# Two mixer layers and an expert block on one core: head 0's q and k turned beside the last projection tiles, scores ahead of head 1's turns

## What is computed

```python
parts = split_in(h @ w_in[l])                      # 21 tiles of 128 columns, and kr
q = mla_q(parts[0], ...); k, v = mla_kv(parts[1], parts[2], ...)   # head norm and rope, 96 wide
z = dwconv(a * sigmoid(g), cf_conv_w) + cf_conv_b
z = silu(layer_norm(z, cf_ln_w, cf_ln_b))
y_c = (z @ cf_pw_w + cf_pw_b) * silu(g_c)
attn = attend(q, concat([kc, k]), concat([vc, v]))  # softmax(q k^T / sqrt(96)) v, per head
x_new = x + gate * (concat([attn * silu(g_a), y_b, y_c]) @ w_out[l])
```

## Time and profile before

| | |
|---|---|
| median of 3 runs | 1403.42 us (1402.58 to 1404.14) |
| the profiled execution | 1405.23 us, its span 1403.4 us, granted clock 0.962 |
| busy: PE, DVE, ACT, POOL | 1301.7, 671.7, 516.1, 581.0 us |
| layer 0: last three tiles, attention | about 254 to 294, 294 to 412 us |
| layer 1: last three tiles, attention | about 637 to 665, 665 to 768 us |

### The profile page before, as it was taken

One profiled execution on the slowest core, in us unless ns is written; L12 is line 12 of the kernel. 1 busy time (PEld: TensorE's weight loads), 2 busy tenths in 40 slices (PEclk: granted clock), 3 DMA queues, 4 the chain that ended last, 5 costly groups with the idle time before them and its releaser, 6 DMA issues. The chain is left out here.

```text
span 1403.4 us, 20309 instructions
## 1 busy us (share of the span) xinstructions
PE 1301.7 (93%) x7696; PEld 940.2 (67%) x7696; DVE 671.7 (48%) x1368; ACT 516.1 (37%) x1062; POOL 581.0 (41%) x599
## 2 busy tenths in 40 slices
PE   4999999989999899989899999999989799999985
PEld 3766877768888877656788987776667653333332
DVE  5456975137751588852675341444353711111216
ACT  4312343246752333523665343565452211111102
POOL 2113698334445446794244431564343311111125
PEclk8999999979999999999899999999989899999998
DMA  8792101130003231112000322221035939999974
GB/s 325 280 338 91 46 31 60 46 150 2 1 24 128 63 114 55 45 61 75 16 2 2 121 91 70 89 98 46 31 125 202 423 125 418 424 425 414 418 317 196
DMA packets 42655, 210.08 MB, mean 150 GB/s; under 512 B 7271, under 2 KB 9703, under 8 KB 33328
## 3 DMA queue, kind: packets, MB, share of 16 engines
q1 hardware_dynamic: 34336, 195.11, 36.3%
q0 software_dynamic: 5760, 10.27, 2.0%
q10 hardware_dynamic: 2448, 3.21, 0.7%
HBM read 201.98 MB, written 17.30 MB: 156 GB/s over the span
## 5 line engine op out<-in xcount | busy, mean ns | idle before, releaser
L436 POOL TENSOR_TENSOR wlo<-raw,whi 128x512 fp32r<-128x512 f32 x112 | 149.7, 1342 | 151.0 <-ACT whi L424 145.6
L3310 PE MATMUL ps<-gu,XT 128*64 128x512 f32 x608 | 136.5, 597 | 5.1 <-DVE XT L3408 3.4
L424 ACT ACTIVATE whi<-raw 128x512 fp32r<-128x512 f32 x124 | 76.5, 628 | 171.9 <-PE ps L872 132.7
L872 PE MATMUL ps<-hxh,whi 128*128 128x512 f32 x304 | 131.0, 431 | 5.0 <-DVE tmpc L1176 4.0
L1138 DVE SCALAR_TENSOR_TENSOR z<-glu,small,z 128x798 f32<-128x798 f32 (+1 forms) x120 | 128.3, 1120 | 0.7
L872 PE MATMUL ps<-hxh,wlo 128*128 128x512 f32 x304 | 121.7, 400 | 1.9 <-POOL wlo L436 1.9
L872 PE MATMUL ps<-hxl,whi 128*128 128x512 f32 x304 | 121.7, 400 | 0.0
L1491 PE MATMUL ps<-kT,qT 96*128 96x256 f32 (+1 forms) x432 | 97.2, 365 | 7.4 <-ACT qT L1537 7.1
L1648 POOL TENSOR_SCALAR P<-P,stat 128x768 f32<-128x768 f32 (+1 forms) x80 | 65.5, 821 | 89.9 <-DVE stat L1610 89.0
L3310 PEld LDWEIGHTS ps<-gu,XT 128*64 128x64 f32 x608 | 45.9, 137 | 82.8 <-issue 75.9
L1546 ACT ACTIVATE P<-ps,stat 128x768 f32<-128x768 f32 (+1 forms) x80 | 65.1, 814 | 66.7 <-DVE stat L1603 66.2
(11 more groups left out here) (846 smaller groups left out, 3096.6 us busy)
## 6 DMA issues: line engine op xcount, KB each, us to landing
gu<-in_w_gu_dram SPq DMA_DIRECT2D x32, 2048.0 KB, 16.4
raw<-in_w_in_dram SPq DMA_DIRECT2D x66, 512.0 KB, 3.4
dn<-in_w_dn_dram SPq DMA_DIRECT2D x32, 1024.0 KB, 16.5
wgate<-in_w_mod_dram SPq DMA_DIRECT2D x16, 1024.0 KB, 8.2
raw<-in_w_out_dram SPq DMA_DIRECT2D x24, 512.0 KB, 3.4
wmod<-in_w_mod_dram SPq DMA_DIRECT2D x4, 2048.0 KB, 13.5
ybuf<-zero SPq DMA_DIRECT2D x1, 4096.0 KB, 12.6
yin<-ybuf SPq DMA_DIRECT2D x4, 1024.0 KB, 8.8
```

What stands on the lines that cost most here:

```text
L424: e.activation(K.hi[i][:, half(h)], K.raw[i % 2][:, half(h)], ACT.Copy).then_inc(*q.up("hi", i, h))
L436: e.tensor_tensor(K.lo[i][:, half(h)], K.raw[i % 2][:, half(h)], K.hi[i][:, half(h)].bitcast(F32), ALU.subtract).then_inc(*q.up("lo", i, h))
L872: p = e.matmul(s[0:m, o:o + n], a, K.h[l, v][x][:, k, :], start=k == 0 and part == 0 and x == 0, stop=end)
L3310: m = e.matmul(s[o, :], x[:, k, o], gu[:, k, :], start=k == 0, stop=k == KT - 1, skip_group_check=True)
```

## The change

- In the job `norm` head 0's k is turned in gap 2 and its q in gap 5 (`turn_pe`), each in one place of `K.px` and as one piece (768 columns, for q in layer 1 512). ScalarE writes the high parts in gaps 3 and 6, VectorE the remainders in gaps 3 and 6, there behind the diagonals. `qs` is computed in gap 1.
- In layer 0 the spread stays in gap 6 and the normed multiply and Silu in gap 7; in layer 1 each comes one gap later. pw stands in gaps 9 and 10 (10 and 11 in layer 1), and what follows it on the other engines one gap after it.
- The splits of the first two tiles of w_out have halves in the order 0, 1.
- A split's event no longer counts as an engine's newest, so a stage mark leaves splits out.
- The attention starts with scores 0. Then come head 1's turns, all pieces, on TensorE and ScalarE; reciprocal 0, the remainders of k, scores 1, reciprocal 1, scores 2, and the other remainders. At u = 0 nothing is turned.
- The places of the scores are those of the ring `K.ps` in its order, so unit 0 gets the one that was evicted first. q and k have a buffer of their own for each head parity and part, and the lifetimes in the memory plan are longer to suit.

```diff
@@ -114,7 +114,9 @@
     def up(self, name, *key):
         base = name.split(".")[0]
         sem = f"{self.engine}_{FAMILY.get(base, base)}"
-        self.newest = (sem, self._count(sem, (name, *key), 1))
+        count = self._count(sem, (name, *key), 1)
+        if base not in ("hi", "lo"):
+            self.newest = (sem, count)
         return self.counts.sem(sem), 1
...
-        ("tmpa", 5 * 3264, 0, 24), ("tmpc", 5 * 3264, 40, 74), ("tmpe", 5 * 3264, 90, 100),
+        ("tmpa", 5 * 3264, 0, 26), ("tmpc", 5 * 3264, 40, 76), ("tmpe", 5 * 3264, 90, 100),
...
-            (f"ga{l}", 4 * r, a + 24, a + 30), (f"gc{l}", 2 * r, a + 24, a + 24),
-            (f"qT{l}", 4 * r, a + 30, a + 30), (f"kT{l}", 4 * row, a + 30, a + 30),
+            (f"ga{l}", 4 * r, a + 24, a + 30), (f"gc{l}", 2 * r, a + 24, a + 26),
+            *[(f"{n}{l}_{b}{p}", s, a + (26, 30)[b], a + 30) for n, s in (("qT", r), ("kT", row)) for b in range(2) for p in "hl"],
...
 def halves_of(i):
 
-    return (1, 0) if any(W_OUT[l] <= i < W_OUT[l] + KT for l in range(2)) else (0, 1)
+    return (1, 0) if any(W_OUT[l] + 2 <= i < W_OUT[l] + KT for l in range(2)) else (0, 1)
...
@@ -940,14 +942,18 @@
                 if k == 1:
                     m.then_inc(*q.up("zsum", l, j))
         yield
+        turn_pe(S, l, K.px, B, 0, 1, 0, 6)
         yield
         yield
         s, before = K.px.take("mean", l, "z")
         sums_pe(S, s, before, B.tmp[3], ("ssq", l, "z"), n_own // 128, [("zsq", l)])
         yield
-        yield
+        turn_pe(S, l, K.px, B, 0, 0, 0, nt_q)
+        for _ in range(1 + l):
+            yield
         s, before = K.px.take("normed", l, 1)
         spread_pe(S, s, before, n_own // 128, B.tmp[4], ("z", l))
+        yield
         yield
         yield
...
         zc = [(c, n, c if c == 0 else c + 30) for c, n in segments(l)]
+        A, free = attention_buffers(K, l), [*after(f"gates{l}"), ("conv", l, 1, 30)]
         yield
...
         yield
-        yield
-        yield
-        yield
-        yield
+        turned_act(S, l, A, 0, 1, 0, NT, free)
+        yield
+        yield
+        yield
+        turned_act(S, l, A, 0, 0, 0, n_own, free)
+        for _ in range(1 + l):
+            yield
...
+        yield
+        yield
         yield
...
     def norm():
         zc = [(c, n, c if c == 0 else c + 30) for c, n in segments(l)]
         s = K.bank["centred", l, 1]
+        A = attention_buffers(K, l)
+        scaled_qs(S, l, A)
         yield
...
         yield
+        turned_dve(S, l, A, 0, 1, 0, NT, [])
         yield
         nt = n_own // 128
         mean_dve(S, K.bank["mean", l, "z"][:, 0:nt], stat[:, 40:40 + nt], 256, LN_EPS, [("ssq", l, "z"), *begin_of(l)], ("mean", l, "z"))
         yield
         yield
         spread_dve(S, stat[:, 48:54], nt, tmp[4], [("root", l, "z"), ("k_rope", 6 * l + 5), ("q_rope", 6 * l + nt_q - 1)], ("z", l))
-        yield
+        turned_dve(S, l, A, 0, 0, 0, n_own, [])
+        for _ in range(1 + l):
+            yield
...
         yield
+        yield
+        yield
         for f in range(2):
...
-        yield
-        yield
-        yield
-        yield
+        for _ in range(6 + l):
+            yield
...
@@ -1386,16 +1403,19 @@
             rests.append((h, which, t0))
             yield
 
-    def finish():
-        while rests:
+    def finish(most=4):
+        for _ in range(min(most, len(rests))):
             rest(*rests.pop(0))
-    for _ in pieces(0):
-        finish()
-    nxt = pieces(1)
-    for u in range(3):
-        scores(u)
-        if u < 2:
-            normalise(u)
+    scores(0)
+    for _ in pieces(1):
+        pass
+    nxt = iter(())
+    normalise(0)
+    finish(2)
+    scores(1)
+    normalise(1)
+    scores(2)
+    finish()
     for u in range(n):
         h, i = units[u]
         if u in due:
@@ -1403,7 +1423,7 @@
         turn_p(u)
         if i < 2:
             next(nxt, None)
-            if i or h == 0:
+            if i:
                 for _ in nxt:
                     pass
         elif i >= per - 2 and h + 2 < HEADS:
...
-    A.qT, A.kT = K.sb(f"qT{l}", [128, 2, 2, n_own], F32R), K.sb(f"kT{l}", [128, 2, 2, NT], F32R)
+    A.qT, A.kT = ([[K.sb(f"{name}{l}_{b}{p}", [128, n], F32R) for p in "hl"] for b in range(2)] for name, n in (("qT", n_own), ("kT", NT)))
...
-    A.S = [K.psum[:, o:o + NT] for o in (0, 1024)]
+    A.S = K.bank.get(("places of scores", l))
...
+def turn_pe(S, l, places, B, h, which, t0, nt):
+
+    K, e, q = S.K, S.e, S.q
+    s, before = places.take("turned_lo", l, h, which, t0)
+    for j in range(nt):
+        i = 6 * l + t0 + j
+        for w in q(*([("kn", i), ("k_rope", i)] if which else [("q_rope", i)]), *before):
+            e.wait_ge(*w)
+        m = e.transpose(s[0:QK, 128 * j:128 * j + 128], (B.qN, B.kN)[which][:, t0 + j, h, :], K.ident[:, :])
+        if j == nt - 1:
+            m.then_inc(*q.up("turned", l, h, which, t0))
+
+
+def turned_act(S, l, A, h, which, t0, n, free):
+
+    K, e, q = S.K, S.e, S.q
+    s = K.bank["turned_lo", l, h, which, t0]
+    dst, weight = ((A.qT, A.qs), (A.kT, small(K, "kh_w", l, 1)))[which]
+    for w in q(("turned", l, h, which, t0), ("qs", l), *free):
+        e.wait_ge(*w)
+    e.activation(dst[h % 2][0][0:QK, 128 * t0:128 * t0 + n], s[0:QK, 0:n], ACT.Copy, scale=weight[0:QK, :]).then_inc(*q.up("turned_hi", l, h, which, t0))
+
+
+def turned_dve(S, l, A, h, which, t0, n, free):
+
+    K, e, q = S.K, S.e, S.q
+    s = K.bank["turned_lo", l, h, which, t0]
+    dst, weight = ((A.qT, A.qs), (A.kT, small(K, "kh_w", l, 1)))[which]
+    hi, lo = (part[0:QK, 128 * t0:128 * t0 + n] for part in dst[h % 2])
+    for w in q(("turned_hi", l, h, which, t0), *free):
+        e.wait_ge(*w)
+    e.scalar_tensor_tensor(lo, s[0:QK, 0:n], weight[0:QK, :], hi.bitcast(F32), ALU.mult, ALU.subtract).then_inc(*q.up("turned_lo", l, h, which, t0))
+
+
+def scaled_qs(S, l, A):
+
+    K, e, q = S.K, S.e, S.q
+    for w in q(("small",), *begin_of(l)):
+        e.wait_ge(*w)
+    e.tensor_scalar(A.qs, small(K, "qh_w", l, 1), float(np.float32(QK) ** np.float32(-0.5)), None, ALU.mult).then_inc(*q.up("qs", l))
+
+
+def slot_free(A, l, h):
+
+    return [("scores", l, A.per * (h - 1) - 1)] if h > 1 else after(f"layer{l}")
+
+
...
+    K.bank["places of scores", l] = [place for place, _ in K.ps.places]
+    s_free = [before for _, before in K.ps.places]
...
-    s_free = [before for i in range(2) for place, before in K.ps.places if place is K.ps_wide[i]]
...
+        turn_pe(S, l, K.G, B, h, which, t0, 4 if t0 == 0 else 2)
...
-                a = A.qT[0:QK, b, qpart, 128 * t:128 * t + 128]
+                a = A.qT[b][qpart][0:QK, 128 * t:128 * t + 128]
...
-                    ready = [(("turned_hi", "turned_lo")[qpart], l, h, 0, i // 4 * 4), (("turned_hi", "turned_lo")[kpart], l, h, 1, 0 if c < NX else 4)]
+                    ready = [(("turned_hi", "turned_lo")[qpart], l, h, 0, i // 4 * 4 if h else 0), (("turned_hi", "turned_lo")[kpart], l, h, 1, 4 if h and c >= NX else 0)]
...
+    K.ps.places = [(A.S[u % 2], (("weights", l, u),)) for u in (len(units) - 2, len(units) - 1)]
...
+        turned_act(S, l, A, h, which, t0, 512 if t0 == 0 else 256, slot_free(A, l, h))
...
-    sm = float(np.float32(QK) ** np.float32(-0.5))
-    for w in q(("small",), *after(f"layer{l}")):
-        e.wait_ge(*w)
-    e.tensor_scalar(A.qs, small(K, "qh_w", l, 1), sm, None, ALU.mult).then_inc(*q.up("qs", l))
...
+        turned_dve(S, l, A, h, which, t0, 512 if t0 == 0 else 256, slot_free(A, l, h))
```

More of the change, by code:

```diff
@@ L287, in setup @@
         items += [
[L288 to L289 removed]
+            (f"hxh{l}", 16 * kb, a if l == 0 else 42, a + 26), (f"hxl{l}", 16 * kb, a if l == 0 else 42, a + 26),
+            (f"hch{l}", 8 * kb, a if l == 0 else 44, a + (26 if l == 0 else 10)), (f"hcl{l}", 8 * kb, a if l == 0 else 44, a + (26 if l == 0 else 10)),
             (f"cqw{l}", 3 * row, a + 10, a + 20), (f"krT{l}", row, a + 10, a + 10), (f"krN{l}", 6 * 32 * 4, a + 10, a + 20),
             (f"wkr{l}", 1024, a + 10, a + 10), (f"wkrh{l}", 1024, a + 10, a + 10), (f"wkrl{l}", 1024, a + 10, a + 10),
[L292 to L293 removed]
+            (f"wuq{l}", 6 * kb, a + 10, a + 20), (f"wukv{l}", 4 * kb, a + 10, a + 20), (f"pw{l}", 2 * kb, a + 10, a + 26),
+            (f"glu{l}", 2 * 828 * 4, a + 10, a + 24), (f"z{l}", 2 * 798 * 4, a + 10, a + 26),
             (f"scp{l}", 2 * 772 * 4, a + 20, a + 20), (f"scz{l}", 772 * 4, a + 20, a + 20),
             (f"qN{l}", nt * 768 * 4, kv, a + 30), (f"kN{l}", 6 * 768 * 4, kv, a + 30), (f"vN{l}", 6 * 512 * 4, kv, a + 30),
[L296 to L297 removed]
+            (f"ga{l}", 4 * r, a + 24, a + 30), (f"gc{l}", 2 * r, a + 24, a + 26),
+            *[(f"{n}{l}_{b}{p}", s, a + (26, 30)[b], a + 30) for n, s in (("qT", r), ("kT", row)) for b in range(2) for p in "hl"],
             (f"P{l}", 4 * row, a + 30, a + 30), (f"PTa{l}", 12 * kb, a + 30, a + 30), (f"PTb{l}", 6 * kb, a + 30, a + 30),
@@ L1466, in turn @@
     def turn(h, which, t0):
```

(40 more changed lines are left out.)

4 lines of the change are left out of this document (removed).

## The result

| | before | after |
|---|---|---|
| median | 1403.78 us (1402.58 to 1404.14) | 1385.22 us (1382.83 to 1387.39, 4 runs) |
| ratio, 95% interval | | 0.9873 [0.9854, 0.9891] |
| the profiled execution | 1405.23 us, clock 0.962 | 1385.88 us, span 1384.1, clock 0.970 |

The change makes the kernel 18.6 us faster.

A forecast was written before the change was run, and what follows sets the result against it. TensorE bounds the steady attention; its idle and slow time sits between projection tiles and attention. Gains 3.9 + 8.1 + 2.8 + 5.9 - 0.7 = 20.0 us off 1403.42 give 1383.4 us, range 1378.5 to 1392.

The forecast's parts named there:

- Tile phase: Last projection tiles before the attention: waits and slow clock at the pw products go, net gain 3.9 and 2.8 us.
- Rival C: Tile phase: Silu is still late and the pw product still waits, 5.17 + 3.91 us stay; 1392.5 us, chance 0.05.
- Scores at once: Start of the attention: scores 0 start within 0.3 us of the last tile's product, exp 0 at 2.8 us.
- E: In times, the last tile's product end; as rival, clock stays low into the attention's steady part, 1413 us, chance 0.04.
- Rival F: Attention opening: first exp still waits for the layer mark, openings start some 3 us later; 1389.4 us, chance 0.05.
- The table load: ScalarE before exp 0: exp table load takes 1.28 us with no drain, against the skill's about 2.66 us.
- Opening: Start of each layer's attention, from the last tile's product to the sixth maximum: gains of 8.1 and 5.9 us.
- Sixth maximum: VectorE's sixth maximum of scores in each opening: about 15.6 and 15.1 us after the last product, before 23.7 and 21.0.
- Low stretches: TensorE's lower clock after idles in the new opening: 0.35 us a layer taken off, bounds nothing to 6.8 in all.
- Rival B: Attention openings: clock stays at the lower level, half the openings' 14 us goes; 1390.4 us, chance 0.20.
- Later stages "as long as before": Stages behind the openings: they were to take as long as before, so the gain would carry through.
- D: Later stages: the expert weight stream's start does not move and absorbs the gain; about 1402 us, chance 0.04.

The follow-up runs named there:

- before_halves: The kernel before with one line changed, the first two w_out tiles' splits taking half 0 first; 1389.06 us, ratio 0.9903 [0.9887, 0.9920].

## Why the prediction was right

The forecast was 1383.4 us against 1385.22 and 1383.22 measured, in the range and on the side of "faster". Step by step:

- **Tile phase, forecast 3.9 and 2.8, measured 4.1 and 3.0.** The order of halves gives 5.4 and 4.1 by itself, the turns cost 1.3 and 1.1, as summed. What the later place of the pw product gives, part of my reason, no run shows: before_halves has no wait without it, but head 0's copies do not stand ahead of Silu there. Rival C is out.
- **Scores at once, right.** The table load started at E + 1.6, exp 0 at 2.9 (2.8 forecast). The last y split of GpSimd ended 0.2 us before E in layer 0 and held the table load up by 0.42 us in layer 1. Rival F did not occur, but it was closer than my 0.05 made it look: it is what the old order of halves brings.
- **The table load** took 1.28 us, and exp 0 began at 293.10, 0.01 us behind its end. The 2.66 us of the Trainium skill (ScalarE: Activation LUTs, "What ACT_TABLE_LOAD costs") would have put it at 294.5; the measurement decides for the row, as the sum did.
- **Opening, mis-sized term.** Sixth maximum forecast at 15.6 and 15.1, measured at 14.1 and 14.2; the stated check of 15 to 17 us is missed on the early side. The second, third and fourth were due at 5.8, 8.0 and 11.0 and came at 5.5, 7.6 and 10.2. First, instructions that follow each other on VectorE start 0.06 to 0.08 us before the recorded end of the one before (the pair of remainders of 1.14 at 294.70 is followed by the maximum at 295.76, a pitch of 1.06), and I had added up durations and rounded them up. The Trainium skill (ScalarE: Activation LUTs, "What ACT_TABLE_LOAD costs") states about 93 ns of such overlap for activations on ScalarE; ScalarE's rows agree (a split of 0.63 at 290.41, the next activation at 290.95), and VectorE's show the same kind of overlap. Second, the short fifth unit took 1.86 us from its maximum to the next (302.49 to 304.35), where I had 2.4. Together that is 1.5 us in layer 0; in layer 1, whose fifth unit is a full one, the first alone is 0.9.
- **Low stretches.** I allowed 0.35 us a layer; one stretch came in layer 0 (298:303), about 1.7 us of clock with no wait of VectorE's maxima for TensorE behind it, and none in layer 1. Rival B would have needed a clock near 0.5 for over 7 us. The attention's steady part is at 1.00 (314:408), so E did not occur.
- **Later stages "as long as before": not quite.** The trace had gained 22.5 us by layer 1's sixth maximum, and the profiled execution 19.35 in the end; D, which had all of the gain absorbed, is out. The forecast sat 2 us from the medians because the openings gave 2.4 us more than summed and the stretches downstream took more than that back. The mechanism held, but that the number came so close is in part luck: two errors of opposite sign.
- **What each part is worth** the sum did not say. Its terms for the opening were made for the whole change, but part of the old opening was lost to the late splits: the one line on halves gives 0.0097 of 0.0130 by the medians and 12.9 of 23.5 us at the seams, and head 0's turns, the marks and the new order share the rest. The terms are not additive, either: taken out of the complete change, the same line costs 0.006, or 10.5 us at the seams.

## What to carry to other kernels

When a step waits long, look what stands ahead of it in its own engine's queue and for what that waits: one prefetch split that waited for a whole product, not for half of it, held up an activation, a matmul and the clock behind it, and mending that order alone brought three quarters of the gain by the medians, a little over half of it at the seams. Read the same question forwards before moving a step to a later gap: what it is put behind may wait for the end of the stage (the y splits behind the last weight split). And where single executions differ by several us in untouched stages, compare the changed stretch between two fixed points of the traces, and repeat an unaltered kernel before calling a difference far away from the change its own.
